# Three feed-forward products by blocks with seven multiplications, hidden tiles made and used in pairs

## The chip, the cores and the metric

The kernel runs on one core of one Trainium2 chip. The metric is the device time of one execution in microseconds. TensorE (PE) multiplies, PEld is its weight load, which overlaps the multiplication; VectorE (DVE), ScalarE (ACT) and GpSimd (POOL) do the elementwise work, and SyncE (SP) issues the transfers (DMA).

## What is computed

Two transformer blocks over 1024 positions of width 1024, all in float32. The parts that the change touches are the two feed-forward networks; D_FF is 2816 and D_FF_2 is 4096:

```python
    # first block
        h2 = rmsnorm(x, norm2_g[l])
        g = jnp.einsum('bsd,df->bsf', h2, w_gate[l])
        u = jnp.einsum('bsd,df->bsf', h2, w_up[l])
        x = x + jnp.einsum('bsf,fd->bsd', jax.nn.silu(g) * u, w_down[l])
    return rmsnorm(x, normf_g)
...
    # second block (w_ff1, w_ff2), followed by a last rmsnorm
    h2 = _rmsnorm(x, g_ffn)
    x = x + jnp.square(jax.nn.relu(h2 @ w_ff1)) @ w_ff2
```

Ahead of each network stands a mixing layer: differential and forget-gate attention in the first block, two convolutions and stick-breaking attention in the second, each closed by a product with w_out and a residual sum.

## The kernel before

**Data.** All activations lie transposed, in 8 tiles of 128 features by 1024 positions. X is the residual stream. R0 and R1 each hold 8 such tiles twice: as a high part (rounded to the float32r format) and a low part (what the rounding left). One product of a weight tile (128 by 128) with half a row of activations (512 positions, `cols(half)`) is three matmuls: high weights by high activations, low weights by high, high weights by low. They are lines 1225, 1228 and 1231.

**Weights.** They come in pieces of four 128x128 tiles (256 KB) into `raw` (3 buffers). ACT rounds a piece into `wh` (L1692) and POOL takes the difference into `wl` (L1864); both have 4 buffers. `load_piece` and `split_piece` keep this a few pieces ahead of PE.

**Feed-forward before.** `ffn` makes hidden tiles in groups (8, 7, 7 of 22 in the first network; 8, 8, 8, 8 of 32 in the second). For each hidden tile, `dense` runs the weight tile over both halves, 8 row tiles each, 24 matmuls to a PSUM bank and 48 to a tile; the banks are evicted by DVE with the factor rstd (gate L1560, up L1566, relu L1585), and the product (L1571) and the low part (L1576, L1589) go back to the free region. Then the group is multiplied into X: for each of 8 output tiles one `dense` over the group's tiles, evicted by `down_evac` (L1539, X <- PSUM + X). In the last group each output tile is followed by its share of the next norm: the high part (ACT L1801), the squares (ACT L1811) summed by POOL into mix (L1910), in the first network also squares with the gain (ACT L1820) summed by DVE into rstd (L1548), and the low part (DVE L1552). The squares go through one buffer, P2.

**The starts of the networks.** `second_pass` adds the last of eight row tiles of w_out into X for each output tile (L1535 evicts), makes the next activations (ACT L1801, DVE L1552) and sums squares, while `start_ffn` already multiplies the first two weight tiles (gate 0 and up 0, or ff1 0 and 1) row tile by row tile. `rsqrt` then turns the sum into rstd (L1379 to L1398); no hidden tile can be evicted before.

**Order.** `work_order` writes the steps in one order. `engine_orders` turns it into a fixed order for each engine with a list schedule over a table of costs, in which the engines don't disturb each other. Each engine then runs its list strictly in order and waits on semaphores. PE's list is the written one, up to small shifts.

## Time and profile before

| | us |
|---|---|
| median of 3 runs (lowest, highest) | 2621.61 (2619.77, 2624.3) |
| the profiled execution's own time | 2624.18 |
| its span | 2622.4 |
| PE busy | 2529.0 (96%) |
| DVE busy | 1193.4 (46%) |
| ACT busy | 911.6 (35%) |
| POOL busy | 831.0 (32%) |

The first network's PE work runs from about 654 to 1388 us, the second's from about 1882 to 2593 us. A matmul is shown as busy for 0.39 us though the next starts 0.23 us later, since they are pipelined; PE's pace is read from starts, not from durations. DVE's durations overlap in the same way by about 0.09 us.

### The profile page before, as it was taken

Reading aid. Unit: us, or ns where it says so; the run is one execution under the profiler, and the core shown is the slowest. Engines: PE = TensorE matmul, PEld = TensorE weight load, DVE = VectorE, ACT = ScalarE, POOL = GpSimd, SP = SyncE. Lnnn points to the kernel's source line nnn. Section 1 sums busy time; section 2 is a strip of 40 time slices with the busy share of each in tenths; the row PEclk is TensorE's granted clock in tenths of the full one; section 3 lists DMA queues with packets and bytes.
Section 4 is the critical chain, followed back from the end, with each engine's and each line's share of the span. In section 5 each row is a group of like instructions: output and inputs, shape, how many; then the busy total and the mean of one; then the engine's idle time right before and its main releaser. Section 6 shows DMA issues by size and latency. Waiting matters only on the chain.

```text
span 2622.4 us, 30803 instructions
## 1 busy us (share of the span) xinstructions
PE 2529.0 (96%) x11910; PEld 2069.6 (79%) x11910; DVE 1193.4 (46%) x1675; ACT 911.6 (35%) x1528; POOL 831.0 (32%) x594
## 2 busy tenths in 40 slices
PE   8999999999999999999999989999999999999996
PEld 6777788878788888888887867887878888888884
DVE  6766667672633123213336997776341121221213
ACT  5455555552522122112244125554241131221321
POOL 4766542212522222222243343331342222222232
PEclk9999999999999999999999989999999999999998
DMA  3311221232111111111112122123111111111111
GB/s 136 85 47 53 83 61 49 59 98 77 46 48 49 49 49 48 47 51 48 47 51 109 57 61 65 54 74 99 61 53 49 48 49 48 49 49 49 49 49 68
DMA packets 85776, 158.63 MB, mean 60 GB/s; under 512 B 10368, under 2 KB 17280, under 8 KB 85504
## 3 DMA queue, kind: packets, MB, share of 16 engines
q1 hardware_dynamic: 85632, 156.67, 19.3%
q8 instruction: 95, 1.56, 0.2%
q14 instruction: 49, 0.40, 0.0%
HBM read 122.55 MB, written 15.20 MB: 53 GB/s over the span
## 4 chain that ended last, share of the span: by engine, by line
PE 84%; DVE 7%; ACT 3%; issue 2%; POOL 2%; DMA 1%; SPq 0%; POOLq 0%; DVEq 0%; ACTq 0%
PE PS L1225 24%; PE PS L1231 24%; PE PS L1228 24%; PE PS L1295 3%; PE PS L1282 2%; PE PS L1316 2%; PE PS L1313 2%; PE PS L1276 2%; DVE R L1552 1%; DVE sm L1452 1%; PE PS L1279 1%; DVE Pb L1466 1%; DVE Pb L1476 1%; POOL wl L1864 0%; POOL mix L1910 0%
## 5 line engine op out<-in xcount | busy, mean ns | idle before, releaser
L1225 PE MATMUL PS<-R,wh 128*128 128x512 f32 x3088 | 1221.4, 396 | 8.9 <-ACT R L1700 4.2
L1231 PE MATMUL PS<-R,wh 128*128 128x512 f32 x3088 | 1208.6, 391 | 4.5 <-DVE R L1552 4.4
L1228 PE MATMUL PS<-R,wl 128*128 128x512 f32 x3088 | 1208.1, 391 | 0.0
L1864 POOL TENSOR_TENSOR wl<-raw,wh 128x512 fp32r<-128x512 f32 (+1 forms) x394 | 523.5, 1330 | 1516.9 <-ACT wh L1692 1516.1
L1231 PEld LDWEIGHTS PS<-R,wh 128*128 128x128 f32 x3088 | 582.5, 189 | 130.8 <-DVE R L1552 6.1
L1225 PEld LDWEIGHTS PS<-R,wh 128*128 128x128 f32 x3088 | 583.3, 189 | 125.8 <-ACT R L1700 4.3
L1228 PEld LDWEIGHTS PS<-R,wl 128*128 128x128 f32 x3088 | 582.9, 189 | 115.1 <-issue 2.9
L1692 ACT ACTIVATE wh<-raw 128x512 fp32r<-128x512 f32 (+1 forms) x394 | 244.9, 622 | 876.4 <-PE PS L1231 873.1
L1539 DVE TENSOR_TENSOR X<-PS,X 128x512 f32<-128x512 f32 x112 | 77.5, 692 | 459.4 <-PE PS L1231 459.4
L1764 ACT ACTIVATE PT<-PS 128x512 fp32r<-128x512 f32 (+1 forms) x200 | 109.1, 554 | 106.8 <-PE PS L1295 98.9
L1276 PE MATMUL PS<-R 128*128 128x512 f32 (+2 forms) x288 | 109.9, 382 | 22.7 <-ACT Pb L1747 9.9
L1295 PE MATMUL PS<-ident,Pb 128*128 128x128 f32 x720 | 109.0, 276 | 9.8 <-DVE PT L1497 4.6
L1282 PE MATMUL PS<-R 128*128 128x512 f32 (+2 forms) x288 | 118.3, 411 | 0.0
L1585 DVE SCALAR_TENSOR_TENSOR stage<-PS,rstd 128x512 f32<-128x512 f32 x64 | 43.9, 691 | 160.6 <-PE PS L1231 160.4
L1295 PEld LDWEIGHTS PS<-ident,Pb 128*128 128x128 f32 x720 | 86.3, 142 | 29.6 <-issue 14.2
L1452 DVE TENSOR_REDUCE sm<-PS 128x1 f32<-128x128 f32 (+7 forms) x128 | 94.9, 750 | 26.3 <-PE PS L1282 25.6
L1476 DVE TENSOR_TENSOR_SCAN Pb<-TABF,vec 128x128 f32<-128x128 f32 (+3 forms) x64 | 93.7, 1472 | 10.6 <-PE PS L1295 7.0
L1566 DVE TENSOR_TENSOR stage<-PS,rstd 128x512 f32<-128x512 f32 x44 | 30.3, 690 | 148.6 <-PE PS L1231 148.6
L1639 DVE SCALAR_TENSOR_TENSOR CV<-CV,vec,CV 128x1024 f32<-128x1024 f32 x64 | 96.6, 1527 | 0.2
L1499 DVE TENSOR_TENSOR PT<-PS,PT 128x512 fp32r<-128x512 f32 (+1 forms) x120 | 75.1, 631 | 41.2 <-ACT PT L1764 40.7
L1313 PE MATMUL PS<-PT,R 128*128 128x256 f32 x480 | 91.8, 287 | 2.1 <-DVE stage L1517 1.1
L1747 ACT ACTIVATE Pb<-PS,sm 128x128 f32<-128x128 f32 (+3 forms) x96 | 71.0, 740 | 57.3 <-DVE sm L1452 56.7
(209 smaller groups left out, 2103.4 us busy)
## 6 DMA issues: line engine op xcount, KB each, us to landing
raw<-w_ff_dram SPq DMA_DIRECT2D x128, 256.0 KB, 2.7
raw<-w_in_dram SPq DMA_DIRECT2D x92, 256.0 KB, 2.7
R<-R SPq DMA_DIRECT2D x96, 128.0 KB, 2.3
raw<-w_gate_dram SPq DMA_DIRECT2D x44, 256.0 KB, 2.6
raw<-w_up_dram SPq DMA_DIRECT2D x44, 256.0 KB, 2.6
raw<-w_down_dram SPq DMA_DIRECT2D x32, 256.0 KB, 2.6
raw<-w_out_dram SPq DMA_DIRECT2D x20, 256.0 KB, 2.8
X<-xT_dram SPq DMA_DIRECT2D x8, 512.0 KB, 8.0
```

Of the source, the lines that this page charges most:

```text
L1225: e.matmul(PS[:, b, :], T.wh[:, h, kc], high, start=(k == 0), stop=False)
L1228: e.matmul(PS[:, b, :], T.wl[:, h, kc], high, start=False, stop=False)
L1231: m = e.matmul(PS[:, b, :], T.wh[:, h, kc], low, start=False, stop=(k == nk - 1))
L1276: e.matmul(S2[:, k0:k1], q, u.KH[:, a, k0:k1], start=True, stop=False)
L1282: m = e.matmul(S2[:, k0:k1], q, u.KL[:, a, k0:k1], start=False, stop=True)
L1295: m = e.transpose(PS[:, s["tb"], at:at + 128], T.Pb[:, s["slot"], par, 128 * kt:128 * kt + 128], T.ident[:, :])
L1313: e.matmul(o, lhs, T.PT[:, x, 0, kk], start=s["first"] and n == 0, stop=False)
L1452: e.reduce_max(sm[:, o + 1:o + 2], S2[:, 0:n], AX, negate=True).then_inc(*sg.up("max", j["key"]))
L1476: e.tensor_tensor_scan(dst[:, ::-1], bt[:, ::-1], T.zeros(n), 1.0, ALU.mult, ALU.add).then_inc(*sg.up("p", j["key"]))
L1692: e.activation(T.wh[:, n % 4, 0:m], T.raw[:, n % 3, 0:m], ACT.Copy).then_inc(*sg.up("w_hi", n))
L1764: e.activation(T.PT[:, s["x"], 0, 0:m], PS[:, s["tb"], 0:m], ACT.Copy, bias=bias).then_inc(*sg.up("pt_hi", key))
L1864: e.tensor_tensor(T.wl[:, n % 4, 0:m], T.raw[:, n % 3, 0:m], T.wh[:, n % 4, 0:m].bitcast(F), ALU.subtract).then_inc(*sg.up("w_lo", n))
```

## The change

**Seven products.** Two weight tiles (gate t and up t, or ff1 t and t+1) over both halves of the positions are read as a product of 2x2 blocks: the row tiles, even and odd, are the inner index, the two weight tiles and the two halves the outer ones. Strassen's scheme (in Winograd's form) makes them with 7 block products in place of 8. A block product is 4 weight tiles over one half: 12 matmuls in one bank, so 84 for a pair of tiles in place of 96. `plan_seven` loads the four weight blocks (every other row tile: `k:8:2`) and has DVE make the sums s1 to s4 (`weight_sum`, L1830 and L1834, in float32, before the rounding). The products come in the order P1, P6, P2, P5, P7, P3, P4 over banks 0 to 2. ACT copies P1 to a stage buffer, and DVE adds each further product to partial sums there (`seven_add`, L1840, 7 for a pair); the results are then scaled by rstd from the stage buffers (gate L1886, up L1895, relu L1915). The activations' four block sums are made once for each network, in R0 (`right_sums`: ACT copies, 16 DVE sums L1852, 16 rounded parts on ACT, 16 low parts on DVE L1859). Tiles 0 and 1 of gate and up, and tiles 0 to 3 of ff1, are still made the old way; 20 pairs in the first network and 14 in the second take the new one.

**Pairs of hidden tiles.** The hidden tiles lie in the quarters of R1 that the block products don't read, room for two tiles (four for the last ones), and each pair is multiplied into X as soon as it is made (`dense_down`: pieces of 2x2 weight tiles, 24 matmuls each, over banks 3 to 7), between the third and the fourth block product of the next pair (`AHEAD`). The last four tiles go in one pass (`dense_last`), with the norm's work behind each output tile. X is evicted to 400 times in both networks, before 112.

**Weight buffers.** `raw` and `wl` become seven buffers `values`; the low part is written over the piece. In the networks two more lie in P2, and mix serves as two more stage buffers. A buffer is taken again when PE has finished with its piece. The regions R0 and R1 change places after the first network.

```diff
-        self.raw = self.new("raw", [128, 3, 512], F, 6144)
         self.wh = self.new("wh", [128, 4, 512], R, 8192)
-        self.wl = self.new("wl", [128, 4, 512], R, 8192)
+        values = self.new("values", [128, 7, 512], F, 14336)
+        lows = self.at("lows", [128, 7, 512], R, self.place["values"])
+        self.wv, self.wl = [values[:, i, :] for i in range(7)], [lows[:, i, :] for i in range(7)]
...
+        self.wv += [late[:, i, :] for i in range(2)]
+        self.wl += [late_r[:, i, :] for i in range(2)]
...
+    def plan_down(self, name, t):
+
+        for e in range(0, 8, 2):
+            self.plan_piece("square", name, e, t, 4, False)
+
+    def plan_seven(self, first, second):
+
+        a11 = self.plan_piece("even", *first, 0, 4, False, turn=False)
+        a21 = self.plan_piece("even", *second, 0, 4, False, turn=False)
+        a22 = self.plan_piece("odd", *second, 1, 4, False, turn=False)
+        a12 = self.plan_piece("odd", *first, 1, 4, False, turn=False)
+        s1 = self.plan_piece("sum", "minus both", 0, 0, 4, False, (a21, a22), False)
+        s2 = self.plan_piece("sum", "minus both", 0, 0, 4, False, (s1, a11), False)
+        s3 = self.plan_piece("sum", "in place", 0, 0, 4, False, (a11, a21), False)
+        s4 = self.plan_piece("sum", "difference", 0, 0, 4, False, (a12, s2), False)
+        a11.read_by, a22.read_by, a12.read_by = [s2, s3], [s1], [s4]
+        s1.read_by, s2.read_by = [s2], [s4]
+        factors = dict(P1=a11, P6=s2, P2=a12, P5=s1, P7=s3, P3=s4, P4=a22)
+        return factors
...
+    def dense_seven(self, t, factors, src, sums, evac, ready=None):
+        right = dict(P1=(src, 0, 0), P2=(src, 1, 0), P3=(src, 1, 1), P5=(sums, 0, 0), P6=(sums, 0, 1), P7=(sums, 1, 0), P4=(sums, 1, 1))
+        stage = {}
+        def add(what, part, to, one, read):
+            new = to not in stage
+            if new:
+                stage[to], gi = self.next_stage()
+            self.step("seven_add", b=b, i=stage[to], k=stage[one], gi=gi if new else [], done=("dense", (t, part)),
+                      read=[("first", t) if r == "S1" else ("seven", (t, r)) for r in read], key=(t, what))
+            return ("seven", (t, what))
+        for name in ("P1", "P6", "P2", "P5", "P7", "P3", "P4"):
+            piece, (region, row, half) = factors[name], right[name]
+            self.split_to(piece)
+            b = self.seven_at % 3
+            self.seven_at += 1
+            given = self.claim(b)
+            for k in range(4):
+                self.mm(b, (region, 2 * k + row, half), piece, k, k == 0, k == 3, given if k == 0 else [],
+                        ready[name][k] if ready else [], [(t, name)] if k == 3 else [], k == 3)
+            self.used = max(self.used, piece.turn + 1)
+            self.last_dense = ("dense", (t, name))
+            if name == "P1":
+                stage["a"], gi = self.next_stage()
+                self.step("seven_copy", b=b, i=stage["a"], gi=gi, done=("dense", (t, name)), key=t)
+                self.bank_given[b] = [("first", t)]
+            elif name == "P6":
+                self.bank_given[b] = [add("S6", name, "b", "a", ["S1"])]
+            elif name == "P2":
+                self.bank_given[b] = [add("C11", name, "a", "a", ["S1", "S6"])]
+                evac("C11", None, stage["a"], [], ("seven", (t, "C11")))
+            elif name == "P5":
+                self.bank_given[b] = [add("S65", name, "c", "b", ["S6"])]
+            elif name == "P7":
+                part = add("S67", name, "b", "b", ["S6", "S65"])
+                self.bank_given[b] = [part, add("C22", name, "d", "c", ["S65"])]
+                evac("C22", None, stage["d"], [], ("seven", (t, "C22")))
+            elif name == "P3":
+                self.bank_given[b] = [add("C12", name, "c", "c", ["S65", "C22"])]
+                evac("C12", None, stage["c"], [], ("seven", (t, "C12")))
+            else:
+                self.bank_given[b] = [add("C21", name, "b", "b", ["S67"])]
+                evac("C21", None, stage["b"], [], ("seven", (t, "C21")))
+            self.split_ahead()
+            yield
...
+SEVEN, AHEAD = ("P1", "P6", "P2", "P5", "P7", "P3", "P4"), 3
+def ffn_order(pairs, downs, need, plain):
+    begun = 0
+    for p in range(downs - 2):
+        while begun <= need(p):
+            yield "seven", begun, 0, 7
+            begun += 1
+        if p < plain:
+            yield "down", p, 0, 0
+            continue
+        yield "seven", begun, 0, AHEAD
+        yield "down", p, 0, 0
+        yield "seven", begun, AHEAD, 7
+        begun += 1
+    for i in range(begun, pairs):
+        yield "seven", i, 0, 7
+    yield "last", downs - 2, 0, 0
...
+    def right_sums(tag, j, gcol, freed):
+        x = [("post_hi", (tag, 2 * j + 1)), ("post_lo", (tag, 2 * j + 1))]
+        O.step("right_z", tag=tag, j=j, gcol=gcol, given=x + freed)
+        for a in (0, 1, 2, 3):
+            O.step("right_sum", tag=tag, j=j, a=a, gcol=gcol, given=x + freed, later=60)
+        for a in (1, 0, 2, 3):
+            O.step("right_hi", tag=tag, j=j, a=a, later=60)
+            O.step("right_lo", tag=tag, j=j, a=a, later=60)
...
+        if t >= last:
+            return places[2 + t % 2][half], [("dense", ((tag, 19 if tag == "n2" else 13), "P1"))]
+        return places[t % 2][half], [("dense", (tag, "down", t // 2 - 1) if t > 1 else "straight " + tag)]
...
+        elif kind == "weight_sum":
+            piece = s["piece"]
+            one, other = piece.sources
+            m, out = slice(0, 128 * piece.m), T.wv[piece.v]
+            for event in s["given"]:
+                w.wait_ge(*sg.at(*event))
+            w.wait_ge(*sg.at(*one.made()))
+            w.wait_ge(*sg.at(*other.made()))
+            if piece.name == "minus both":
+                i = e.scalar_tensor_tensor(out[:, m], T.wv[one.v][:, m], -1.0, T.wv[other.v][:, m], ALU.mult, ALU.subtract)
+            else:
+                if piece.name == "in place":
+                    w.wait_ge(*sg.at("w_sum", piece.n - 1))
+                i = e.tensor_tensor(out[:, m], T.wv[one.v][:, m], T.wv[other.v][:, m], ALU.subtract)
+            i.then_inc(*sg.up("w_sum", piece.n))
...
+            elif piece.kind == "square":
+                src = weights[c:c + 2, :, k:k + 2, :].rearrange("e p k c -> p e k c")
+            elif piece.kind == "tile":
+                src = weights[c, :, k:k + m, :]
+            else:
+                src = weights[c, :, k:8:2, :]
```

**What moves on DVE, 1: the start of a network.** The rows are DVE's list in `second_pass` of w_out in the first block, from its middle to the mean of the squares. L1535 (after: L1820) evicts X, L1552 (L1876) is the low part of the activations. Before:

```order
L1552 SCALAR_TENSOR_TENSOR R_50<-X,vec,R_50 128x1024
L1535 TENSOR_TENSOR X<-PS,XP_76 128x512 x2
L1552 SCALAR_TENSOR_TENSOR R_50<-X,vec,R_50 128x1024
L1535 TENSOR_TENSOR X<-PS,XP_76 128x512 x4
L1552 SCALAR_TENSOR_TENSOR R_50<-X,vec,R_50 128x1024 x2
L1379 TENSOR_SCALAR stage<-PS 128x512 x2
```

After, from the same place:

```order
L1876 SCALAR_TENSOR_TENSOR R_50<-X,vec,R_50 128x1024
L1820 TENSOR_TENSOR X<-PS,XP_77 128x512 x2
L1859 TENSOR_TENSOR R_49<-R0f,R_49 128x512 x2
L1876 SCALAR_TENSOR_TENSOR R_50<-X,vec,R_50 128x1024
L1820 TENSOR_TENSOR X<-PS,XP_77 128x512 x2
L1859 TENSOR_TENSOR R_49<-R0f,R_49 128x512
L1852 SCALAR_TENSOR_TENSOR R0f<-X,vec,R0f 128x512
L1876 SCALAR_TENSOR_TENSOR R_50<-X,vec,R_50 128x1024
L1852 SCALAR_TENSOR_TENSOR R0f<-X,vec,R0f 128x512 x3
L1859 TENSOR_TENSOR R_49<-R0f,R_49 128x512 x4
L1664 TENSOR_SCALAR stage<-PS 128x512 x2
```

Ten instructions of the block sums (L1852, L1859) stand ahead of the last L1876, and seven more between it and the mean of the squares (L1664); the second network has the same ten and seven.

**What moves on DVE, 2: between two passes into X.** After the change DVE's list in the middle of the first network reads, from one pass into X through the four block products behind it:

```order
L1863 TENSOR_TENSOR X<-PS,X 128x512 x16
L1830 SCALAR_TENSOR_TENSOR values<-values 128x512
L1840 TENSOR_TENSOR stage<-PS,mix 128x512
L1830 SCALAR_TENSOR_TENSOR values<-values,late 128x512
L1834 TENSOR_TENSOR values<-late,values 128x512
L1840 TENSOR_TENSOR mix<-PS,mix 128x512
L1840 TENSOR_TENSOR stage<-PS,stage 128x512
L1834 TENSOR_TENSOR values<-values 128x512
L1895 TENSOR_TENSOR stage<-stage,rstd 128x512
```

Before, the same stretch of work was four rows to a tile:

```order
L1560 TENSOR_TENSOR stage<-PS,rstd 128x512 x2
L1566 TENSOR_TENSOR stage<-PS,rstd 128x512
L1571 TENSOR_TENSOR stage<-stage 128x512
L1576 TENSOR_TENSOR R_49<-stage,R_49 128x512
L1566 TENSOR_TENSOR stage<-PS,rstd 128x512
```

The 16 evictions into X (L1863) now follow one another with nothing between, the four weight sums stand behind them, and the scaling reads stage buffers where it read PSUM.

**What moves on DVE, 3: the end of the first network.** Before, each output tile's two evictions (L1539), its low part (L1552) and its sum (L1548) alternate. After, in the last pass:

```order
L1863 TENSOR_TENSOR X<-PS,X 128x512 x3
L1876 SCALAR_TENSOR_TENSOR R_49<-X,sm,R_49 128x1024
L1872 TENSOR_TENSOR rstd<-rstd,P_61 128x1024
L1863 TENSOR_TENSOR X<-PS,X 128x512
L1935 MEMSET CV_79 128x32
L1935 MEMSET CV_80 128x32
L1935 MEMSET CV_83 128x32
L1876 SCALAR_TENSOR_TENSOR R_49<-X,sm,R_49 128x1024
L1872 TENSOR_TENSOR rstd<-rstd,P_61 128x1024 x3
L1664 TENSOR_SCALAR stage<-PS 128x512 x2
```

The last three sums (L1872) now stand together behind the last low part, so the schedule has three of them still open when the last eviction is done.

## Rows read from the trace of the kernel before

**Rows 1.** The page: busy time by engine, and the chain that ended last.

```profile
PE 2529.0 (96%) x11910; PEld 2069.6 (79%) x11910; DVE 1193.4 (46%) x1675; ACT 911.6 (35%) x1528; POOL 831.0 (32%) x594
PE 84%; DVE 7%; ACT 3%; issue 2%; POOL 2%; DMA 1%; SPq 0%; POOLq 0%; DVEq 0%; ACTq 0%
```

**Rows 2.** Busy time by stretch: length, PE, PEld, DVE, ACT, POOL, PEclk, DMA share, GB/s.

```profile
720.00:1388.00 668.00, 668.00 (x2949) 553.31 (x2948) 179.22 (x220) 151.85 (x228) 174.68 (x133) 1.00 0.16 49
...
1450.00:1500.00 50.00, 50.00 (x223) 41.39 (x222) 48.89 (x43) 5.69 (x9) 16.23 (x10) 1.00 0.20 64
```

**Rows 3.** PE's timeline, two matmuls that are 86 apart: start, us, what.

```profile
1329.69 0.39 PE L1225 MATMUL PS<-R,wh 128*128 128x512 f32 x1
...
1349.18 0.39 PE L1231 MATMUL PS<-R,wh 128*128 128x512 f32 x1
```

**Rows 4.** Groups by line and shape, 720 to 1320 us: x, busy us, mean ns.

```profile
L1864 POOL TENSOR_TENSOR wl<-raw,wh 128x512 fp32r<-128x512 f32 x102 | 131.9, 1293 | 446.9 <-ACT wh L1692 446.9
L1692 ACT ACTIVATE wh<-raw 128x512 fp32r<-128x512 f32 x103 | 65.1, 632 | 247.3 <-PE PS L1231 247.3
L1571 DVE TENSOR_TENSOR stage<-stage 128x512 f32<-128x512 f32 x40 | 48.0, 1201 | 4.2
```

**Rows 5.** Timelines of DVE and POOL in the first network, around 704 and 954 us.

```profile
703.05 1.28 DVE L1566 TENSOR_TENSOR stage<-PS,rstd 128x512 f32<-128x512 f32 x2
703.80 1.30 POOL L1864 TENSOR_TENSOR wl<-raw,wh 128x512 fp32r<-128x512 f32 x1 [2.64 <-ACT wh L1692]
953.94 1.30 POOL L1864 TENSOR_TENSOR wl<-raw,wh 128x512 fp32r<-128x512 f32 x1 [1.43 <-ACT wh L1692]
954.04 1.75 DVE L1571 TENSOR_TENSOR stage<-stage 128x512 f32<-128x512 f32 x1
970.36 0.69 DVE L1571 TENSOR_TENSOR stage<-stage 128x512 f32<-128x512 f32 x1
```

**Rows 6.** DMA issues, 630 to 660 us: x, KB each, median us to landing.

```profile
raw<-w_gate_dram SPq DMA_DIRECT2D x3, 256.0 KB, 2.6
raw<-w_out_dram SPq DMA_DIRECT2D x1, 256.0 KB, 2.8
```

**Rows 7.** Start of the first network: busy time by stretch; PE's waits, 650 to 720.

```profile
660.00:691.40 31.40, 30.03 (x130) 24.15 (x129) 21.18 (x18) 16.14 (x18) 27.85 (x13) 1.00 0.11 36
PE PS L1231 <- DVE R L1552: 2.2, 2, 1.4
```

**Rows 8.** DVE's and POOL's timeline there: last low part, last sum, mean, rstd, first evictions.

```profile
682.93 3.51 DVE L1552 SCALAR_TENSOR_TENSOR R<-X,vec,R 128x1024 fp32r<-128x1024 f32 x1 [1.08 <-ACT R L1801]
691.36 0.69 DVE L1379 TENSOR_SCALAR stage<-PS 128x512 f32<-128x512 f32 x1 [4.92 <-PE PS L1249]
701.85 1.29 DVE L1560 TENSOR_TENSOR stage<-PS,rstd 128x512 f32<-128x512 f32 x2
686.52 2.41 POOL L1910 TENSOR_TENSOR mix<-mix,P 128x1024 f32<-128x1024 f32 x1 [1.17 <-ACT P L1811]
```

**Rows 9.** One output tile of the last group: squares and sums through P2, four timelines.

```profile
1333.09 1.04 ACT L1811 ACTIVATE P<-X 128x1024 f32<-128x1024 f32 x1
1334.21 2.56 POOL L1910 TENSOR_TENSOR mix<-mix,P 128x1024 f32<-128x1024 f32 x1 [1.29 <-ACT P L1811]
1336.81 1.15 ACT L1820 ACTIVATE P<-X,vec 128x1024 f32<-128x1024 f32 x1 [2.67 <-POOL mix L1910]
1337.99 1.22 DVE L1548 TENSOR_TENSOR rstd<-rstd,P 128x1024 f32<-128x1024 f32 x1 [1.29 <-ACT P L1820]
```

**Rows 10.** DVE's timeline, end of the first network to the first convolution eviction; PE's waits.

```profile
1388.37 0.69 DVE L1539 TENSOR_TENSOR X<-PS,X 128x512 f32<-128x512 f32 x1 [1.56 <-PE PS L1231]
...
1395.10 1.22 DVE L1548 TENSOR_TENSOR rstd<-rstd,P 128x1024 f32<-128x1024 f32 x1 [3.47 <-ACT P L1820]
...
1425.24 1.28 DVE L1612 TENSOR_TENSOR CV<-PS,rstd 128x512 f32<-128x512 f32 x2
PE PS L1225 <- DVE stage L1388: 2.2, 1, 2.2
```

549 lines of the change are left out of this document (371 added, 178 removed).

## The prediction

> **What bounds the kernel now.** The page comes first: PE is busy 96% of the span, and the chain that ended last is PE for 84% of it [rows 1]. PE's count and pace therefore set the time wherever PE never waits. The view by stretches shows where that is. From 720 to 1388 us, nearly the whole first network, PE is busy all of 668.00 us while DVE has 179 and POOL 175 [rows 2]; the second network looks the same. PE's own timeline gives the pace: 86 matmuls in 19.49 us, 0.2266 us each [rows 3], and 2949 matmuls at that pace fill the 668 us. So inside the networks time is matmuls times 0.2266, as long as the other engines keep up.
>
> Two other readings matter, since the change gives DVE and POOL more to do. First, they get in each other's way. L1571 takes 0.69 us alone at 970.36, but 1.75 at 954.04, where POOL's L1864 runs from 953.94 for 1.30: DVE ends 0.55 us after POOL does, so it was held until POOL had finished. The two evictions from PSUM at 703.05 take 1.28 together though POOL works from 703.80: an operation with one operand in PSUM isn't held [rows 5]. The mean of L1571, 1201 ns, says that about half of them meet a split [rows 4]. The Trainium skill has this as a rule ("SBUF — State Buffer", section "SBUF: two separate sides"): GpSimd shares an exclusive port pair with a VectorE operation that reads two operands from SBUF. The trace agrees, and by the rule as by the rows it bears on every new DVE operation that reads only SBUF.
>
> Second, the starts and the end of the networks. From 660 to 691.4 us POOL is busy 27.85 of 31.40 us [rows 7], and the last low part takes 3.51 us, for 1.2 of work, across POOL's sum at 686.52 [rows 8]. PE waits for these low parts, if only 2.2 us [rows 7]. This stretch has no room on DVE and POOL.
>
> **The matmuls removed.** A pair of tiles takes 84 matmuls in place of 96, and 20 + 14 = 34 pairs are made so: 34 x 12 = 408 fewer. The passes into X keep their count. 408 x 0.2266 = **92.5 us** off.
>
> **The steady stretch.** A block product is 12 x 0.2266 = 2.72 us, a group of seven 19.0, a pass into X 96 matmuls, 21.8. DVE operations on 128x512 follow each other in 0.60 us (the two at 703.05 take 1.28, 0.69 of it the last one's own duration) [rows 5]. For a group DVE has 7 additions from PSUM (4.2 us) and 12 operations on SBUF alone: 4 weight sums, 4 scalings, 2 products and 2 low parts, or 4 low parts (7.2 us). POOL has 7 splits of 1.29 (9.0 us) [rows 4]. What excludes each other is 9.0 + 7.2 = 16.2 of 19.0 us. It fits; and if DVE could do nothing at all beside POOL, 20.4, it would fall 1.4 us behind in a group and catch up in the next pass, where 16 evictions (9.6 us) and 4 splits (5.2) stand against 21.8. ACT has 7 splits at 0.63 [rows 4] and five to nine other operations of that kind, 8 to 10 of 19 us.
>
> What PE waits for has slack. A bank of the seven comes round after two other products, 5.4 us. A pass into X evicts four banks as PE finishes them 0.68 us apart, and each is wanted 12 matmuls, 2.7 us, after it is done, with nothing else between in DVE's order after the change. The hidden tile made last has 3 products, 8.2 us, for an addition, a scaling, a product, a rounding and a low part, 5 x 0.7 = 3.5 and waits. A block of weights is split 3 products ahead; the sum for P6 gets its buffer when P5 of the group before is done, 4 products or 10.9 us early, for about 0.7 + 0.63 + 1.29 and one hold of 1.3. The loads take every other row tile, so in chunks of 512 bytes. The w_out piece across four tiles has such chunks and lands in 2.8 us, where whole pieces land in 2.6 [rows 6]: nothing. I take **2 us** for small holds, bounds 0 and 34 x 1.4 = 48.
>
> **The start of the first network.** Ten of the block sums' operations now precede the last low part. In 660 to 691.4 POOL's own work is 7 sums of 2.4 and 6 splits of 1.29, 24.5 us, and DVE's six low parts 7.2: 31.7 in 31.4, a full port. So the ten add 10 x 0.60 = 6.0 us before PE has its last row tile. Seven more precede the mean of the squares: 17 x 0.6 = 10.2. Before, the mean came at 691.36 and the first eviction at 701.85 [rows 8]; after, the first eviction comes at about 712, which is 19.5 us after the last low part (686.4 before, 692.4 now). PE has 2.7 us of that row tile, then 96 matmuls of gate 1 and up 1, 21.8, and about 0.9 for the sums: P1 would start at 25.4. Its bank 0 holds a half of up 1, and that eviction stands 18 operations behind rstd in DVE's list, at 0.68 each with handovers 12.3, with two or three splits in between 15: 19.5 + 15 = 34.5, so PE waits **9 us**. P6's block sums come 6 operations later, and PE needs its last row 4.7 us later, so that wait takes no more. Start: 6 + 9 = **15 us**, bounds 4 (the ten fill DVE's waits for ACT, P1 waits little) and 24.
>
> **The start of the second.** The same ten and seven operations, so the same 6 us. Behind it stand tiles 2 and 3, then a pass into X at 25.4, which needs tiles 0 and 1: rstd at 19.5, ten operations, the first low part at about 26.8. Then bank 3 must be evicted (2 us) and the pass's own evictions stand behind eight operations (1 us). 1.5 + 2 + 1 and a hold: 5. **11 us**, bounds 3 and 18.
>
> **The end of the first network.** Each output tile sends squares through P2: ACT from 1333.09, POOL, ACT, DVE to 1339.21, 6.1 us in series [rows 9]. Before, a tile came each 9.5 us, and the last sum ended 8 us after PE's last matmul (about 1388.3; 1395.10 + 1.22) [rows 10]. Now a tile is 24 matmuls, 5.4 us, the first two come together, and seven passes through P2 are 43 us and more from about 4.5 us after those two; PE takes 32.6 for the other six. The last sum ends 4.5 + 43 - 32.6 = 15 us after PE, 7 later than before, and a split on ACT or POOL inside each pass adds up to 1 us each, 14 later. That moves the convolutions' first eviction (1425.24 before). PE has about 8 us of banks in hand there, but DVE is then busy 48.89 of 50 us [rows 2], and work that starts late ends late, where the next attention waits for it. I take **8 us**, bounds 0 (hidden by the banks) and 14. At the end of the second network the chain has no second sum, 3.7 us against 5.4: nothing, and the tail after PE stays.
>
> **The sum.** 92.5 - 15 - 11 - 8 - 2 = 56.5 us. The profiled execution took 2624.18 us of its own, 2567.7 after; the median of the runs is 2.6 below it, so **2565**. With all lower costs it is 2621.6 - 85.5 = 2536; with the upper ones at the starts and the end (56) and 2 inside, 2587.
>
> **The rivals.**
> (A) The starts and the end hide their work: DVE waits there for ACT (1.08 us before the last low part [rows 8]), and sums may slip in. For: PE waited only 2.2 us. Against: the full port. Costs of 7 to 20: 2536 to 2549, say 2545.
> (B) DVE and POOL become the bound in the groups of seven: holds aren't made good in the pass, each group costs 1.4 us: 34 x 1.4 = 48 in place of 2, **2611**. For: 16.2 of 19.0 us is close. Against: the slack of 5 to 10 us. The skill's rule, in which the loser is blocked for the whole instruction, is what this case follows at its worst.
> (C) Slower: the weight sum for P6 comes late. It is made of two sums in a row, then rounded, then split, on three engines in fixed order; if DVE stands behind in each group and POOL's splits stretch, PE waits in each. It is slower from 56.5 / 34 + 0.1, 1.7 us for each group, on. The chain is about 4 us and has 10.9, so it would have to come 8.6 us late in each: at 10 us late, 3 us x 34 = 102 - 2, **2665**.
> (D) The halved loads land late. They would need over 8 us where 2.8 is shown; 1 in 50, near 2600.
>
> **How the numbers follow.** The forecast 0.63, with 2552 to 2585 as its own range; A 0.15; B 0.14; D 0.02; C 0.05 with a time above 2627; 0.01 for landing level. About 0.2%, 5 us, is what a measurement of this kernel can tell. Faster 0.94, the same 0.01, slower 0.05. The range takes in A from 2542 and part of the way to B, 2595: it leaves out C, D and most of B, under 2 in 10.
>
> **What would show it.** 8856 matmuls of the three dense lines (before 9264) at 0.2266. In the middle of both networks PE busy without waits (steps 1 and 2 right); waits of PE for L1840, L1863 or for the splits would be B or C. At the starts a wait for the low part of about 8 us and one for the eviction of up 1 of about 9. At the end of the first network the last sum L1872 some 15 us or more behind PE's last matmul of the pass. The prediction is wrong if the starts cost nothing or twice as much, or if the convolutions absorb the late rstd.

## The result and the profile after

The changed kernel takes 2556.8 us (median of 4 runs, 2555.6 to 2557.7) where the kernel before, timed beside it, takes 2620.7: a ratio of 0.9754, 95% interval 0.9737 to 0.9770, 63.9 us less. The forecast was 2565 with an own range of 2552 to 2585, so the time is 8 us below the forecast and inside the range. The profiled execution took 2557.67 us of its own, with a span of 2555.9.

The page of the kernel after, to be held against [rows 1] and the counts of [rows 4]:

```profile
PE 2436.8 (95%) x11502; PEld 1991.5 (78%) x11502; DVE 1755.1 (69%) x2401; ACT 999.0 (39%) x1700; POOL 1029.4 (40%) x692
...
PE 83%; DVE 9%; ACT 3%; issue 2%; POOL 1%; DMA 1%; SPq 0%; POOLq 0%; DVEq 0%; ACTq 0%
...
L1516 PE MATMUL PS<-R,wh 128*128 128x512 f32 x2952 | 1170.2, 396 | 22.5 <-DVE stage L1673 8.0
L1521 PE MATMUL PS<-R,wh 128*128 128x512 f32 x2952 | 1157.5, 392 | 14.3 <-DVE R L1876 14.2
L2215 POOL TENSOR_TENSOR lows<-values,wh 128x512 fp32r<-128x512 f32 (+1 forms) x420 | 610.2, 1456 | 1116.7 <-ACT wh L2023 1011.6
```

PE still bounds the kernel, and the dense lines have 3 x 2952 = 8856 matmuls, 408 fewer, as counted. The largest entries of their idle time name two places where PE waits: low parts of h (L1876) and rstd behind the first network (L1673).

The view by stretches of the kernel after, columns as in [rows 2]:

```profile
700.00:716.00 16.00, 14.65 (x65) 11.82 (x63) 14.38 (x22) 10.90 (x17) 1.59 (x1) 1.00 0.07 19
717.00:727.00 10.00, 4.87 (x12) 3.81 (x13) 10.00 (x14) 3.86 (x7) 3.92 (x3) 0.50 0.00 1
740.00:1300.00 560.00, 560.00 (x2473) 463.84 (x2472) 389.77 (x507) 161.97 (x266) 253.87 (x172) 1.00 0.18 54
```

Inside the first network (third row) PE is busy all of 560 us with 2473 matmuls, 0.2264 us each: the steady stretch holds, though DVE is now busy 70% of it. The second row is the wait at the first group of seven and the matmuls just behind it; the granted clock over it is 0.50, the 1.2 GHz level.

PE's waits of the kernel after at the start of the first network (640 to 800 us) and of the second (1840 to 1960), us in total, times, longest; the answer to [rows 7], where 2.2 us stood:

```profile
PE PS L1521 <- DVE R L1876: 7.6, 4, 2.8
PE PS L1516 <- DVE stage L1895: 7.5, 1, 7.5
...
PE PS L1521 <- DVE R L1876: 6.3, 4, 2.9
PE PS L1516 <- DVE stage L1915: 2.0, 1, 2.0
```

The places are those that the prediction named: the low parts (L1876) and, in the first network, the eviction of up 1 (L1895).

The last passes into X and what follows, PE's timeline of the kernel after (start, us, what, idle before it):

```profile
1365.87 3.52 PE L1534 MATMUL PS<-mix,ones 128*128 128x512 f32 x4 [3.82 <-issue]
1379.09 0.80 PE L1516 MATMUL PS<-R,wh 128*128 128x512 f32 x1 [7.98 <-DVE stage L1673]
```

The mean of the last squares waits for the chain through P2, and then PE waits 7.98 us for L1673, a scaling on the way to the second of two inverse roots that stand in a row there, where it waited 2.2 before [rows 10].

### The profile page after: what moved, and what is told of

Same layout as the page of the kernel before. It is cut to its first block, busy times and chain, and to the rows that moved or that the text cites. A ratio compares the mean times of both kernels' runs of the same rounds, so it can differ in the third digit from the quotient of the medians.

```text
span 2555.9 us, 30901 instructions
## 1 busy us (share of the span) xinstructions
PE 2436.8 (95%) x11502; PEld 1991.5 (78%) x11502; DVE 1755.1 (69%) x2401; ACT 999.0 (39%) x1700; POOL 1029.4 (40%) x692
## 4 chain that ended last, share of the span: by engine, by line
PE 83%; DVE 9%; ACT 3%; issue 2%; POOL 1%; DMA 1%; SPq 0%; POOLq 0%; DVEq 0%; ACTq 0%
PE PS L1516 24%; PE PS L1521 24%; PE PS L1518 23%; PE PS L1580 3%; PE PS L1567 2%; PE PS L1601 2%; PE PS L1598 2%; PE PS L1561 2%; DVE R L1859 1%; DVE R L1876 1%; PE PS L1564 1%; DVE Pb L1751 1%; DVE sm L1737 1%; DVE Pb L1749 1%; DVE X L1820 1%
## 5 line engine op out<-in xcount | busy, mean ns | idle before, releaser
L1516 PE MATMUL PS<-R,wh 128*128 128x512 f32 x2952 | 1170.2, 396 | 22.5 <-DVE stage L1673 8.0
L1521 PE MATMUL PS<-R,wh 128*128 128x512 f32 x2952 | 1157.5, 392 | 14.3 <-DVE R L1876 14.2
L2215 POOL TENSOR_TENSOR lows<-values,wh 128x512 fp32r<-128x512 f32 (+1 forms) x420 | 610.2, 1456 | 1116.7 <-ACT wh L2023 1011.6
L1518 PE MATMUL PS<-R,lows 128*128 128x512 f32 x2588 | 1014.9, 392 | 1.1 <-POOL lows L2215 1.1
L1518 PEld LDWEIGHTS PS<-R,lows 128*128 128x128 f32 x2588 | 490.1, 189 | 97.4 <-issue 2.4
L2023 ACT ACTIVATE wh<-values 128x512 fp32r<-128x512 f32 (+1 forms) x420 | 261.8, 625 | 762.4 <-PE PS L1521 704.0
L1863 DVE TENSOR_TENSOR X<-PS,X 128x512 f32<-128x512 f32 x400 | 273.0, 691 | 248.4 <-PE PS L1521 248.4
L1840 DVE TENSOR_TENSOR stage<-PS,stage 128x512 f32<-128x512 f32 x153 | 104.1, 688 | 102.5 <-PE PS L1521 102.3
L2215 POOL TENSOR_TENSOR late_r<-late,wh 128x512 fp32r<-128x512 f32 x72 | 108.2, 1504 | 135.8 <-ACT wh L2023 96.6
L1518 PE MATMUL PS<-R,late_r 128*128 128x512 f32 x364 | 141.6, 389 | 0.0
L1737 DVE TENSOR_REDUCE sm<-PS 128x1 f32<-128x128 f32 (+7 forms) x128 | 95.0, 751 | 29.1 <-PE PS L1567 28.5
L1784 DVE TENSOR_TENSOR PT<-PS,PT 128x512 fp32r<-128x512 f32 (+1 forms) x120 | 75.2, 632 | 38.6 <-ACT PT L2110 38.1
L2262 POOL TENSOR_TENSOR mix<-mix,P 128x1024 f32<-128x1024 f32 x28 | 75.7, 2705 | 49.8 <-ACT P L2157 49.8
```

The lines of the kernel that those rows point to most:

```text
L1516: e.matmul(PS[:, b, :], wh, high, start=s["start"], stop=False)
L1518: e.matmul(PS[:, b, :], wl, high, start=False, stop=False)
L1521: m = e.matmul(PS[:, b, :], wh, low, start=False, stop=s["stop"])
L1737: e.reduce_max(sm[:, o + 1:o + 2], S2[:, 0:n], AX, negate=True).then_inc(*sg.up("max", j["key"]))
L1840: e.tensor_tensor(stage[s["i"]], PS[:, s["b"], :], stage[s["k"]], ALU.add).then_inc(*sg.up("seven", s["key"]))
L1863: e.tensor_tensor(x, PS[:, s["b"], :], x, ALU.add).then_inc(*sg.up("x", s["key"]))
```

## Where the time went, stage by stage

The kernel before was profiled once more (run e9 below), and that execution is the fairer one to compare with. Each length runs between starts of evictions in the traces, in us; the last column is the change less 0.2266 for each matmul removed there (240 and 168), so a cost is positive.

| stage | before | before again | after | after - again | cost beside the matmuls |
|---|---|---|---|---|---|
| up to the first second-pass eviction | 654.3 | 651.2 | 650.1 | -1.1 | |
| from there to the last eviction into X, first network | 734.1 | 734.0 | 695.5 | -38.6 | +15.8 (forecast 15, and 1 inside) |
| to the second network's first second-pass eviction | 493.4 | 492.1 | 498.4 | +6.3 | +6.3 (forecast 8) |
| second network | 711.2 | 711.2 | 682.9 | -28.3 | +9.8 (forecast 11, and 1 inside) |
| tail | 29.4 | 29.4 | 29.1 | -0.3 | |

The changes sum to -62.0 = 2555.9 - 2617.9, the difference of the two spans.

## The experiments

All times are medians but that of e9, a single execution; kernels of one group ran on one chip beside the kernel before. That kernel's median was 2620.7 to 2622.1 in the different groups, so a difference between kernels of two groups is uncertain by some 1.5 us, and the ratios are the safer numbers. "Cost" of a network is its stage length as in the table, less that of before and less the matmuls removed.

**e1_pairs_alone and e1b_pairs_all_banks: the pairs without the seven.**

```
-                factors.append(O.plan_seven(*pairs[i]))
...
+                factors.append(pairs[i])
+                O.plan_tile(*pairs[i][0], 0, 8)
+            if n1 == 7:
+                O.plan_tile(*pairs[i][1], 0, 8)
...
-                    runs[i] = O.dense_seven((tag, i), factors[i], 1, 0, evacs(i), first_ready(tag) if i == 0 else None)
...
+                    run(O.dense(*factors[i][x], 0, 8, 1, evacs(i)[x], skip=(0, 1) if i == final else (1,)))
```

> The pairs without the seven: each tile of gate, up and ff1 by its usual eight row tiles (24 matmuls for a half of the tokens, accumulated in one bank and evicted from it with rstd), no block sums, no weight sums, no additions; the passes into X stay those of the changed kernel. Left out: the products never read the quarter of h that holds the hidden tiles now (the row tile beside it is read in its place), and the last pair's products read only the other row tiles, so its output is not the reference's. 9264 dense matmuls again. Theory 1 (the whole gain is the matmuls, the starts cost about 25 us for block sums and a full DVE, pairs and small passes are worth nothing but the later end of the first network, +5): 2556.8 + 92.5 - 25 = 2624, between 2617 and 2631, level with before. Rival (the order in pairs by itself brings or costs something, and the seven more or less than counted): off by more than 8 us from 2621, on the low side if passes of two tiles with banks used at once help, on the high side if they hurt.

Measured 2637.9, ratio 1.0067 (1.0050 to 1.0084), on the rival's high side. The network stages were 738.4 and 719.2 us, and PE waited in short pieces for evictions. In the second network a start comes 1.2 us after the one before it about every 88 us, once in two rounds of a pass and its products:

```profile
PE PS L1517 <- DVE stage L1916: 4.2, 5, 0.9
PE PS L1522 <- DVE R L1877: 2.2, 2, 1.3
PE PS L1517 <- DVE mix L1916: 1.9, 3, 0.9
```

(PE's waits of this kernel, 1887 to 2606 us.) L1916 is an eviction of ff1: a product got a bank that had been filled just before, because passes and products took turns by different lists. That need not belong to pairs, so it was run again with one rotation of banks: `O.dense_banks = list(range(8))` in the passes too, where e1 has `[3, 4, 5, 6, 7]`.

> The pairs without the seven once more, with one difference: the banks go round through all eight in products and passes alike. In the first form passes used banks 3 to 7 and products all eight, and PE's starts show some 20 gaps of 0.5 to 1.24 us in the two networks, where a product took the bank that the pass had just filled. Left out as there: the quarter of h that holds the hidden tiles is never read (the row tile beside it is), so the output is not the reference's. Theory 1 (those gaps were this kernel's own, and pairs cost nothing but the later end of the first network): stage lengths of before, 734 and 711 us, plus 4 in the middle, less the 3 at the start: 2622, between 2618 and 2626. Rival (pairs in short passes cost DVE time of their own, 12 us of it in the networks): 2632 or more.

Measured 2623.7, ratio 1.0008 (0.9999 to 1.0017), as Theory 1 said; stages 733.3, 498.3 and 710.8. Pairs, passes of two tiles and the other place for the hidden tiles cost the networks nothing. The middle is 6.2 us longer than in e9, all that the changed kernel has there: the late end of the first network belongs to the small passes, not to the seven. The whole gain is the seven's.

**e2_no_block_sums.**

```
-        for j in range(4):
-            right_sums(tag, j, gcol, freed + ([O.last_dense] if j == 3 else []))
...
-        right = dict(... P5=(sums, 0, 0), P6=(sums, 0, 1), P7=(sums, 1, 0), P4=(sums, 1, 1))
+        right = dict(... P5=(src, 1, 0), P6=(src, 1, 1), P7=(src, 1, 0), P4=(src, 1, 1))
```

> The seven without the block sums of h: the four products that read sums read a quarter of h itself, so none of the 40 operations on DVE and 40 on ACT for each network is there, and the output is not the reference's. Everything else, the weight sums and the additions too, stays. Theory 1 (block sums ahead of the last low part and of rstd cost 6 to 7 us in each network, and stand before the evictions that PE waits for): the first second-network numbers of before come back, wait for the eviction of up 1 nearly gone, 2556.8 - 15.8 - 9.8 + 2 to 5 left for a full DVE = about 2534, 2530 to 2541. Rival (the starts cost because of what else changed there: other bank order, a pass into X or a product that wants its banks early): less than 8 us lower, above 2549.

The number of operations in this expectation is wrong: a network has 32 of them on DVE and 20 on ACT. Measured 2531.6, ratio 0.9661 (0.9646 to 0.9675), 25.2 us below the changed kernel and as Theory 1 said. The stages are 679.0 and 672.7 us, which is 734.0 and 711.2 less 55.1 and 38.5; that is the 240 and 168 matmuls to within 1 us. PE's waits of this kernel from 640 to 800 us:

```profile
PE PS L1518 <- DVE R L1873: 2.2, 2, 1.4
```

That is the 2.2 of [rows 7] back. So all of the starts' cost is the block sums; the seven additions, weight sums and splits cost nothing there.

**e3_four_more and e3_eight_more: how much room a group has.** More operations on SBUF alone, in the same order of instructions: in each group one weight sum is made three times and two are made twice; with eight more, two are made four times and one three times.

```
+                for r in range(1 if sg.log else 3 if one.kind == "even" else 2):
...
+                    i = e.scalar_tensor_tensor(out[:, m], T.wv[one.v][:, m], -1.0, T.wv[other.v][:, m], ALU.mult, ALU.subtract)
...
+                for r in range(1 if sg.log or piece.name == "in place" else 2):
...
+                    i = e.tensor_tensor(out[:, m], T.wv[one.v][:, m], T.wv[other.v][:, m], ALU.subtract)
```

> The changed kernel with four more VectorE operations on SBUF alone in each group of seven (one weight sum made three times, two made twice; same result), 34 x 4 = 136 in all, in the same order of instructions. Theory 1 (port and DVE in a group: 16.2 of 19.0 us are taken, 2.8 are free, and the pass into X catches up): 16.2 + 2.4 = 18.6, so no more than 5 us longer, 2557 to 2562. Rival (the port is already the edge: DVE operations of 1.2 us each beside POOL): each of the four costs what it takes, 34 x 4 x 0.6 to 1.2 = 82 to 163 us, 2639 and more; in between, 34 x 1.4 = +48, is the case that the prediction called B.

> The same with eight more in each group (one sum four times, one four, one three). Theory 1: 16.2 + 4.8 = 21.0 of 19.0 us, 2.0 over in each group; in the second network a pass of 21.8 us with 14.8 us of DVE and POOL work follows each group and takes 2 up, in the first a pass follows two groups, 4.0 over against 7 spare; only waits inside a group show: 10 us longer, 0 to 34. Rival: what is over is lost, 34 x 2.0 = 68, or more if each operation costs its own time (136 x 2 x 0.6 = 163).

Measured: four more 2559.8, 3 us above the changed kernel; eight more 2616.2, ratio to before 0.9982 (0.9973 to 0.9992), 59.4 us above. The first is as Theory 1 said; the second is outside it and close to the rival's 68. Groups by line and shape from 740 to 1300 us show how the room went (count, busy us, mean ns, idle before them). The changed kernel:

```profile
L1863 DVE TENSOR_TENSOR X<-PS,X 128x512 f32<-128x512 f32 x140 | 95.6, 692 | 81.7 <-PE PS L1521 81.7
L1840 DVE TENSOR_TENSOR stage<-PS,stage 128x512 f32<-128x512 f32 x87 | 59.2, 688 | 55.1 <-PE PS L1521 55.1
...
L1840 DVE TENSOR_TENSOR mix<-PS,mix 128x512 f32<-128x512 f32 x33 | 22.7, 689 | 24.4 <-PE PS L1521 24.2
...
L1840 DVE TENSOR_TENSOR stage<-PS,mix 128x512 f32<-128x512 f32 x9 | 6.1, 682 | 3.0 <-PE PS L1521 3.0
```

With four more in each group (the same lines are L1871 and L1848), and its stretch:

```profile
L1871 DVE TENSOR_TENSOR X<-PS,X 128x512 f32<-128x512 f32 x143 | 97.7, 692 | 76.8 <-PE PS L1521 76.8
L1848 DVE TENSOR_TENSOR stage<-PS,stage 128x512 f32<-128x512 f32 x87 | 58.7, 682 | 2.9 <-PE PS L1521 2.5
...
L1848 DVE TENSOR_TENSOR mix<-PS,mix 128x512 f32<-128x512 f32 x32 | 21.8, 683 | 0.2
```

```profile
740.00:1300.00 560.00, 560.00 (x2472) 463.72 (x2471) 472.39 (x584) 158.98 (x266) 256.96 (x171) 1.00 0.18 53
```

With eight more, two of the lines, the stretch and PE's waits in it:

```profile
L1871 DVE TENSOR_TENSOR X<-PS,X 128x512 f32<-128x512 f32 x144 | 96.3, 689 | 67.1 <-PE PS L1521 67.1
...
L1848 DVE TENSOR_TENSOR stage<-PS,stage 128x512 f32<-128x512 f32 x77 | 51.9, 682 | 0.4
```

```profile
740.00:1300.00 560.00, 543.12 (x2342) 436.58 (x2341) 483.68 (x620) 141.26 (x244) 244.26 (x158) 1.00 0.17 50
```

```profile
PE PS L1516 <- DVE stage L1848: 11.7, 19, 1.0
PE PS L1516 <- DVE mix L1848: 4.7, 7, 1.0
```

An idle time before an addition (L1840) is DVE waiting for PE: it is DVE's room inside a group. It is 82.5 us in the three rows. 560 us hold some 19 groups (two groups and a pass take 2 x 19.0 + 21.8 us): about 4.3 us a group. The four extra operations took it nearly all, 3.1 us left in the whole stretch, and PE still never waited. They cost DVE 82.6 us (472.39 - 389.77) for 77 operations, 1.07 us each, not the 0.60 of the prediction; that price includes the longer holds of the operations beside them. Eight then ask for 8.6 us where 4.3 are free: 4.3 over, and the first network grew by 37.7 / 20 = 1.9 us a group, the second by 21.0 / 14 = 1.5. PE then waits for the additions that free its banks, as the rows of L1848 say. The rest was made up for in the passes, but not all of it, though DVE had time to spare there: it still sat idle for 67.1 us before the evictions into X, where it was 81.7 in the changed kernel. What PE has waited for inside a group can't be caught up behind it.

The waits' own sum in that stretch, 16.4 us, is less than the 131 matmuls missing from it (2473 less 2342), 29.7 us, since a wait delays more than the row counts. By the starts, the 26 waits and the two starts behind each come 25.8 us late together, 1.0 us for each where the rows give 0.6; eighteen more starts come late with next to no wait shown.

**e5_sums_after_low: the ten operations moved out of the way.**

```
-        x = [("post_hi", (tag, 2 * j + 1)), ("post_lo", (tag, 2 * j + 1))]
+        x = [("post_hi", (tag, 7)), ("post_lo", (tag, 7))]
```

> The changed kernel, its block sums held back until the last low part of h is made, in both networks. Correct as it is. Step under test: ten of their operations ahead of the last low part cost 6.0 us in each network. Theory 1 (they do, but in the first network DVE has the same list to get through before the product of the second weight sum, so the time comes back as a later wait there; in the second a pass into X lies between and hides them): first network 0 to -2, second -4 to -6, total 2551, 2549 to 2555. Rival A (the ten are the whole cost): -6 in both, 2545. Rival B (the sums now stand ahead of the evictions of gate 1 and up 1, in both): no better than now, 2556 or more.

Measured 2557.8, ratio 0.9754 (0.9738 to 0.9771): no change, rival B. The first network is 2.2 us shorter than in the changed kernel, the second 0.9 longer. PE's waits of this kernel from 640 to 800 and from 1820 to 1960 us:

```profile
PE PS L1516 <- DVE stage L1895: 11.6, 1, 11.6
PE PS L1521 <- DVE R L1876: 2.2, 2, 1.3
...
PE PS L1516 <- DVE X L1863: 6.5, 1, 6.5
PE PS L1521 <- DVE R L1876: 2.2, 2, 1.4
PE PS L1516 <- DVE stage L1915: 1.8, 1, 1.8
```

The low parts are no longer late, and the time comes back in other waits: 11.6 in place of 7.5 us for the eviction of up 1, and 6.5 for an eviction of the pass, where the changed kernel had none.

**e6_pass_first.** A pass into X ahead of the first group in the first network too.

```
-    ... factors1, 11, need1, 0, "w_down"
+    ... factors1, 11, need1, 1, "w_down"
```

> The changed kernel with the first pass into X ahead of the first group of seven in the first network too, as the second network has it: 21.8 us of matmuls that want no block sum and not the bank of up 1. Correct as it is. Theory 1 (the 7.5 us wait for the eviction of up 1 and the 2.4 us of half clock behind it go, the six of the late low parts stay, and the pass wants its hidden tiles some 2 to 3 us early): first network from 15.8 to 8 or 9 of cost, total 2549.5, 2547 to 2553. Rival (the wait only changes its name: rstd is late, and the hidden tiles of the pass come as late as the eviction did): 2555 to 2560.

Measured 2560.6, ratio 0.9767 (0.9752 to 0.9781), the rival, just beyond its edge; the first network is 2.3 us longer than in the changed kernel. PE's waits, 640 to 800 us:

```profile
PE PS L1516 <- ACT R L2177: 10.3, 1, 10.3
PE PS L1521 <- DVE R L1876: 6.3, 4, 2.8
```

The wait for the eviction became one for a hidden tile (L2177 rounds it), since both stand behind the same rstd and the same block sums.

**e4_own_buffer: the squares with gain out of P2.**

```
-                w.wait_ge(*sg.at("acc2", (name, k)))
-                e.activation(T.P2[:, 0:S], x, ACT.Square, scale=gain2)
+                if k > 2:
+                    w.wait_ge(*sg.at("accg_sum", (name, k - 2)))
+                e.activation(T.SG[:, 1 + 2 * (k % 2), :], x, ACT.Square, scale=gain2)
```

> The changed kernel with the squares with gain at the end of the first network in two buffers of their own (row tiles of h that no product reads any more), so that they no longer take turns in P2 with the plain squares. Correct as it is. Theory 1 (seven turns through P2 of 6 us each set the last sum; ACT to POOL alone is 3.7 us for each tile and less than the 5.4 us in which PE makes one): the last sum from 20.2 to 8 to 12 us behind PE's last eviction. Of the 12.3 us that it came later, 4.9 were left at the second network's start, so some 4 come back: 2553, 2551 to 2555. Rival (the convolutions and the attention set that stretch by DVE's own work, and the 4.9 are something else's): the last sum early as said, but the time within 1 us of 2556.8.

Measured 2548.1, ratio 0.9718 (0.9704 to 0.9733), 8.7 us below the changed kernel, twice what was expected and below Theory 1's range. PE's waits from 1280 to 1420 us, where the changed kernel had 8.0 for L1673, 3.8 of issue and 0.4:

```profile
PE PS L1517 <- ACT R L2148: 4.7, 1, 4.7
PE PS L1517 <- DVE stage L1674: 0.4, 1, 0.4
```

The last sum ends 6.6 us behind the last eviction (20.2 in the changed kernel), though that eviction itself comes 7.4 us later, since DVE now works through the sums between them. The second network starts 9.0 us earlier after the same start of the first. So the chain through P2 cost 9 us. The stretch had grown by 6.3 (table), so the chain accounts for all of that; the other 2.7 would stand in the kernel before as well, which no run of that kernel with a separate buffer shows.

**e7_sums_after_rstd: block sums last of all, with a pass ahead, on top of e4.**

```
-        x = [("post_hi", (tag, 2 * j + 1)), ("post_lo", (tag, 2 * j + 1))]
+        x = [("post_hi", (tag, 7)), ("post_lo", (tag, 7))] + O.rstd_ready
```

> The kernel with separate buffers for the squares (2548.1 measured), with two changes at the starts: a pass into X ahead of the first group in both networks, and all block sums held back until rstd is made. Correct as it is. Theory 1 (the starts are set by the sum of DVE's work between the first row tile and the first evictions of that pass, which must come after the block sums because they overwrite X; the order only renames the wait): the waits for low parts shrink to 2.2 us in each network, a wait for the hidden tiles of the pass or its banks grows by as much; within 4 us of 2548, 2545 to 2552. Rival (43 us of matmuls now stand between the last low part and the first product that wants a block sum, which is room enough for 32 operations): 6 us less in each network, 2536 to 2541.

Measured 2566.6, ratio 0.9790 (0.9776 to 0.9805), 18.5 us above e4: both theories missed. PE's waits from 640 to 800 us:

```profile
PE PS L1517 <- ACT R L2179: 13.4, 1, 13.4
PE PS L1517 <- DVE stage L1887: 6.4, 1, 6.4
PE PS L1522 <- DVE R L1877: 2.2, 2, 1.4
```

and the stretches of e4 and then of this kernel:

```profile
650.00:688.00 38.00, 33.03 (x135) 25.68 (x134) 37.54 (x35) 22.85 (x27) 26.61 (x12) 0.96 0.12 38
...
700.00:740.00 40.00, 32.53 (x131) 26.34 (x130) 34.03 (x47) 19.35 (x33) 10.77 (x7) 0.87 0.12 33
```

```profile
650.00:688.00 38.00, 35.80 (x155) 28.66 (x154) 27.48 (x25) 21.03 (x23) 29.45 (x15) 1.00 0.16 51
...
700.00:740.00 40.00, 20.14 (x68) 15.37 (x67) 35.06 (x52) 18.00 (x32) 4.72 (x3) 0.66 0.04 13
```

The second network had a pass ahead in e4 already, so its 9.7 us more (692.6 against 682.9) are the holding back alone; the first, with both changes, is 8.1 longer. DVE is busy 37.5 of the first 38 us in e4 and 27.5 here. While PE gets its row tiles a little sooner, DVE stands idle for 10 us that the block sums used, and has them still to do when PE waits for it; the matmuls behind the two long waits run at half clock besides (0.66 over the stretch).

**e8_no_low_sums: half of the block sums' DVE work.**

```
-            O.step("right_lo", tag=tag, j=j, a=a, later=60)
...
+            if src == 0 and piece.kind in ("even", "odd", "sum"):
+                low = high
```

> The changed kernel without the low parts of the block sums: the products that want them read the high part twice, so matmuls are as many and the output is not the reference's. 16 of the 32 DVE operations of the block sums in each network are gone. All 32 were worth 16.5 us in the first network and 10.2 in the second. Theory 1 (each operation costs DVE time, about the same each): half of it, 8 and 5, and a little more since the sums that are left stand ahead of the evictions either way: 2543, 2539 to 2547. Rival (only the ten that stand ahead of the last low part and the wait of the first bank count, as steps of fixed size): less than 6 us off, 2551 or more.

Measured 2550.4, ratio 0.9732 (0.9716 to 0.9748): 6.4 us off, between the two. The first network gained 7.0 us, about the share expected; the second only 1.1. PE's waits from 640 to 740 us:

```profile
PE PS L1522 <- DVE R L1877: 7.7, 4, 2.8
```

The wait for up 1's eviction is gone in full, that for the low parts is not: the sums that are left still stand ahead of them. The trace says how many: ten block sums stand ahead of the last low part here too, in both networks, and they take DVE 14.8 us where the ten of the changed kernel take 12.5.

**e9_before_again.**

> The kernel before, unchanged, profiled once more. In its first profile the first eviction of the second pass came at 654.3 us, in the changed kernel and in all experiments made from it between 649.3 and 651.4, though nothing that the change touches runs there. Theory 1 (the clock that TensorE was granted in the first microseconds and at about 240 us differed in that one execution): now between 649 and 652. Rival (the other buffers for weights let the loads or splits of the first stages run earlier): 654 again.

One execution: 2619.7 us, span 2617.9, and the first second-pass eviction at 651.2 us. The rival is refuted, since the buffers are those of before; the 3.1 us belong to the first profile's own execution. That the clock caused them is not shown. Both executions have the same spell at half clock near 240 us, the first and then this one, 2 us earlier:

```profile
240.00:242.00 2.00, 2.00 (x5) 0.84 (x3) 1.93 (x6) 0.00 (x0) 0.73 (x1) 0.50 0.90 221
```

```profile
238.00:240.00 2.00, 2.00 (x5) 0.97 (x5) 1.93 (x5) 0.00 (x0) 0.10 (x1) 0.50 0.89 209
```

The same DVE instructions start 0.6 us apart in the two from 12 us on, 1.6 from about 75, 2.0 from 270 to 545 and 3.1 from 565 on, so the spell adds next to nothing. What differed at these places stays open.

## Why the prediction was right, point by point

**The matmuls removed.** Right: 8856 are there, and e2 against e9 gives 55.1 and 38.5 us for 240 and 168 of them (computed 54.4 and 38.1). e1b shows that nothing else of the change brings time.

**The steady stretch.** The forecast of 2 us was close (about 0 measured), its working was not. It counted what DVE and POOL exclude each other from: "16.2 of 19.0 us", with 0.60 for each operation on SBUF. What runs out first is DVE's own time, with its holds behind splits: one more operation costs 1.07 us, and 4.3 us a group are free (e3). The claim that DVE, once behind in a group, would "catch up in the next pass" failed in size: with eight more, 1.5 to 1.9 of 4.3 us over were lost in each group. So rival B's mechanism is there, but it begins only beyond four more operations a group. Rivals C and D never showed: PE shows no wait at all between 730 and 1338 us, nor between 1914 and 2526.

**The start of the first network.** Forecast 15, measured 15.8. The two waits stand where they were placed: the low parts end 6.2 us later after the stage's start (forecast 6.0), and PE waits 7.5 us for up 1's eviction (forecast 9). The 9 was 1.5 too much. Not foreseen were the matmuls behind the second wait: 12 of them started 0.43 us apart in place of 0.2266, which is 2.4 us. Together 5.4 (7.6 less the 2.2 of before) + 7.5 + 2.4 = 15.3, against 15.8 of the table.

The size of the 6 was luck. The prediction has "the ten add 10 x 0.60 = 6.0 us before PE has its last row tile", on the reading that DVE and POOL filled the stretch between them ("a full port"). The view of the stretch from the first eviction to the end of the last low part, before and after, says otherwise:

```profile
654.30:686.44 32.14, 29.98 (x131) 24.14 (x129) 26.84 (x25) 19.12 (x21) 24.34 (x11) 1.00 0.16 50
```

```profile
650.08:688.39 38.31, 30.77 (x131) 23.80 (x129) 38.08 (x36) 23.40 (x30) 26.30 (x11) 1.00 0.12 35
```

DVE was idle for 5.3 of 32.1 us and is idle for 0.2 of 38.3 now. From start to start the ten operations take it 12.5 us, 1.25 each on average and not 0.60; these two take 3.40 together:

```profile
661.61 3.40 DVE L1852 SCALAR_TENSOR_TENSOR R0f<-X,vec,R0f 128x512 f32<-128x512 f32 x2
```

They cost twice what was counted; 5.1 us of that went into idle time of DVE, which that reading had ruled out (it is rival A's mechanism), and the other operations took 1.3 less. What is left is 6.1: two errors that cancel. Nor are the ten a price of their own: e5 took them away and gained nothing, e6 put a pass ahead of the next wait and lost 4 (2.3 in the first network itself), and e7 held all sums back and lost 18 against e4. The cost is that of 32 operations on a DVE that they leave hardly any free time from the first row tile to the first product; the order decided where PE waits, and holding them all back was worse, since idle time went unused. e2 shows both waits to be the sums' own, and e8, in this network, 7.0 of 16.5 us for half of the operations.

**The start of the second.** Forecast 11, measured 9.8, by the same cause: 4.1 more for low parts, 2.0 for an eviction, and 14 matmuls at 0.43 us (2.9) make 9.0. e8 gained only 1.1 here, which isn't half. PE's waits for low parts grew (to 9.2 us from 1820 to 1960 us, from 6.3), since the ten sums ahead of the last low part took 2.3 us more than the changed kernel's ten; only what stands behind it became less, and that was worth 2.0 us of waiting here against 7.5 in the first network.

**The end of the first network.** Forecast 8, measured 6.3 against e9 (4.9 against the first profile). The last sum ends 20.2 us behind the last eviction, as forecast ("15 us or more"), against 7.95. e4 confirms the chain: freed of P2, the second network starts 9 us earlier. The last sum is 12.3 us later than before, inside the forecast's 7 to 14, and half of that is taken up until the second network starts; the prediction took 8.

**The sum.** It was made for the profiled execution, 2567.7 us, and that took 2557.67. Of the 10.0 us, 4.5 were in the first profile of before, whose span is 2622.4 where e9's is 2617.9; 1.7 are the middle, 2.2 the second network with its steady stretch, 1.1 the stages ahead of the first network, where the change leaves the work as it was, and 0.5 the first network and the tail. Rival A, that starts and end hide their work, did not come true in the time, though DVE's waits took in some 5 us of the sums at each start.

## What to carry to other kernels

When work is added to an engine that is full in a stretch, price the whole list between its first input and the next engine's first need; moving it about only renames the wait, and holding it back can waste idle time that it would have used. Measure an engine's room inside the tight stretch as its idle time before the operations that wait for PE, and price what is added by the durations that operations have beside the other engine; here a dose of known extra operations found the edge (four for 3 us, eight for 59) where a sum of lone durations had the price of one at 0.60 for 1.07. Where two chains take turns in one buffer, ask after every change in the rate of tiles whether the turns are still shorter than a tile: e4's separate buffer is worth some 9 us, and with it the kernel takes 2548.1 us, less than either version compared here.

## What was not expected of the hardware

A wait of PE costs more than itself. PE's timeline of the changed kernel behind the wait for up 1's eviction:

```profile
722.13 0.80 PE L1516 MATMUL PS<-R,wh 128*128 128x512 f32 x1 [7.48 <-DVE stage L1895]
722.72 0.63 PE L1518 MATMUL PS<-R,lows 128*128 128x512 f32 x1
723.15 0.63 PE L1521 MATMUL PS<-R,wh 128*128 128x512 f32 x1
723.58 0.63 PE L1516 MATMUL PS<-R,wh 128*128 128x512 f32 x1
```

They start 0.43 us apart, at a granted clock of 0.50, the 1.2 GHz level, and the pace of 0.2266 returns after 12 of them. At the starts of all these kernels each of the eleven waits of 4.6 us and more has 7 to 14 such matmuls behind it. Of the twenty waits between 2.3 and 3 us, twelve have 6 to 14 and eight have none, among them the ones of 2.85 us at 674.2 and 2.41 at 683.8 in the changed kernel. In e2, without such waits, no matmul of a product starts so at either start. (The four matmuls that sum the squares, L1249 before and L1534 after, start 0.43 to 0.6 us apart at a granted clock of 1.00 and are not counted.)

A separate buffer makes two chains overlap and then hold each other. The sum into rstd, 128x1024 with both operands in SBUF, took 1.2 us while it took turns with POOL's sum, and 2.6 once both ran freely; the changed kernel and then e4, the line's minimum, median and maximum in ns:

```profile
L1872 DVE TENSOR_TENSOR rstd<-rstd,P x7: 1212/1225/1711, 1322.4 to 1364.5; 128x1024 f32<-128x1024 f32 x7
```

```profile
L1873 DVE TENSOR_TENSOR rstd<-rstd,SG x7: 2216/2646/3415, 1319.8 to 1357.7; 128x1024 f32<-128x1024 f32 x7
```

Each of e4's seven sums ends 1.1 us after the sum of POOL's that runs when it starts, and the split that POOL starts meanwhile takes 2.3 us for 1.3. The separate buffers still paid, since the turns had been longer. The additions from PSUM (L1840, L1848), in contrast, kept 0.68 to 0.69 us at every dose of e3.

The Trainium skill ("SBUF — State Buffer", section "SBUF: two separate sides") gives GpSimd and a VectorE operation that reads two operands from SBUF one exclusive port pair; both rows agree with it.
